# First modulation of a hybrid gMLP/HGRN2 layer: from four passes of 2 MB weight tiles to four chunks of 512 features, with the first projection interleaved

## The reference, cut to what matters

```
sh1, sc1, ... = split(silu(c) @ w_ada + b_ada, 6)       # c for latent, c_ctx for context
h_lat = rms_norm(x)   * gain * (1 + sc1)  + sh1
h_ctx = rms_norm(ctx) * gain * (1 + csc1) + csh1
U, V, Q, I, FF, FB, G = split(h @ w_in)                   # 7 x 1024 columns
mix = concat(gmlp(U, V), hgrn2(Q, I, FF, FB, G))          # context needs only I, FF, FB
x = x + g1 * (mix @ w_out)
x = x + g2 * (relu(h2 @ w_ff1)^2 @ w_ff2),  h2 = modulated rms_norm(x)
out = rms_norm(x) * final_gain
```

## Time and profile before

| | |
|---|---|
| median of 3 runs | 2718.37 us (2716.9 to 2723.17) |
| span of the profiled execution | 2717.8 us |
| TensorE busy | 2563.4 us (94%) |
| GpSimd busy | 1000.9 us (37%) |
| VectorE busy | 1246.9 us (46%) |
| ScalarE busy | 727.6 us (27%) |
| moved | 354.70 MB, mean 131 GB/s |

### The profile page before, as it was taken

One profiled execution on the slowest core, in us unless ns is written; L12 is line 12 of the kernel. 1 busy time (PEld: TensorE's weight loads), 2 busy tenths in 40 slices (PEclk: granted clock), 3 DMA queues, 4 the chain that ended last, 5 costly groups with the idle time before them and its releaser, 6 DMA issues.

```text
span 2717.8 us, 33317 instructions
## 1 busy us (share of the span) xinstructions
PE 2563.4 (94%) x12240; PEld 2111.8 (78%) x12240; DVE 1246.9 (46%) x1463; ACT 727.6 (27%) x929; POOL 1000.9 (37%) x420
## 2 busy tenths in 40 slices
PE   4789999999999999998899999999999999999997
PEld 0479787777777887787788888888888888888886
DVE  0476447788888523666423223332332333323224
ACT  1344222222222223223321322212222222231222
POOL 0330243323232343343344444444444444444442
PEclk9899999999999999999999999999999999999998
DMA  9734454333443452364133323232322322232322
GB/s 411 279 121 163 165 192 150 131 123 123 134 144 124 141 208 93 114 229 153 62 101 109 101 93 102 93 101 94 99 96 97 98 94 100 94 101 93 102 93 101
DMA packets 104769, 354.70 MB, mean 131 GB/s; under 512 B 9936, under 2 KB 10192, under 8 KB 100688
## 3 DMA queue, kind: packets, MB, share of 16 engines
q1 hardware_dynamic: 104224, 352.46, 38.1%
q10 hardware_dynamic: 432, 0.54, 0.1%
HBM read 348.77 MB, written 4.19 MB: 130 GB/s over the span
## 4 chain that ended last, share of the span: by engine, by line
PE 55%; issue 29%; POOL 10%; DMA 3%; DVE 2%; ACT 1%; POOLq 0%; SPq 0%; DVEq 0%; ACTq 0%
POOL w_lo L313 10%; PE bank L1108 9%; PE bank L1109 9%; PE bank L1110 9%; PE bank L1122 9%; PE bank L1123 9%; PE bank L1124 9%; DMA ada_w<-in_w_ada 3%; DVE prep_tmp L669 0%; DVE x_tok L659 0%; DVE x_res L1056 0%; PE bank L1068 0%; ACT junk L393 0%; DVE g_tmp L1034 0%; PE bank L1157 0%
## 5 line engine op out<-in xcount | busy, mean ns | idle before, releaser
L313 POOL TENSOR_TENSOR w_lo<-raw,w_hi 128x1024 fp32r<-128x1024 f32 x416 | 1000.7, 2406 | 1691.7 <-ACT w_hi L346 1691.7
L346 ACT ACTIVATE w_hi<-raw 128x1024 fp32r<-128x1024 f32 x448 | 475.5, 1062 | 1681.4 <-PE bank L1110 870.9
L1108 PE MATMUL bank<-h_hi,w_hi 128*128 128x512 f32 x1696 | 673.6, 397 | 3.4 <-POOL w_lo L313 2.9
L1109 PE MATMUL bank<-h_lo,w_hi 128*128 128x512 f32 x1696 | 663.7, 391 | 0.0
L1110 PE MATMUL bank<-h_hi,w_lo 128*128 128x512 f32 x1696 | 663.6, 391 | 0.0
L1122 PE MATMUL bank<-w_hi,hid_hi 128*128 128x512 f32 x1024 | 398.3, 389 | 0.0
L1123 PE MATMUL bank<-w_lo,hid_hi 128*128 128x512 f32 x1024 | 398.3, 389 | 0.0
L1124 PE MATMUL bank<-w_hi,hid_lo 128*128 128x512 f32 x1024 | 398.3, 389 | 0.0
L1108 PEld LDWEIGHTS bank<-h_hi,w_hi 128*128 128x128 f32 x1696 | 321.1, 189 | 69.8 <-POOL w_lo L313 3.4
L1110 PEld LDWEIGHTS bank<-h_hi,w_lo 128*128 128x128 f32 x1696 | 320.4, 189 | 68.0
L1109 PEld LDWEIGHTS bank<-h_lo,w_hi 128*128 128x128 f32 x1696 | 321.2, 189 | 63.6
(11 more groups left out here) (182 smaller groups left out, 2089.0 us busy)
## 6 DMA issues: line engine op xcount, KB each, us to landing
raw<-in_w_stream SPq DMA_DIRECT2D x448, 512.0 KB, 3.5
ada_w<-in_w_ada SPq DMA_DIRECT2D x128, 512.0 KB, 4.1
ada_w<-in_w_ada SPq DMA_DIRECT2D x16, 2048.0 KB, 18.0
x_tok<-in_x SPq DMA_DIRECT2D x4, 1024.0 KB, 27.1
x_res<-in_x SPq DMA_DIRECT2D x4, 1024.0 KB, 12.1
out<-x_res SPq DMA_DIRECT2D x4, 1024.0 KB, 4.0
ctx_tok<-in_ctx_x SPq DMA_DIRECT2D x2, 1024.0 KB, 16.5
fin_row<-in_final_row SPq DMA_DIRECT2D x1, 1024.0 KB, 7.0
```

The lines of the kernel that those rows point to most:

```text
L313: pool.tensor_tensor(w_lo[:, r % 2], raw[:, r], w_hi[:, r % 2].bitcast(F32), ALU.subtract).then_inc(lo_done, 1)
L346: act.activation(w_hi[:, r % 2], raw[:, r], ACT.Copy).then_inc(hi_done, 1)
L1108: pe.matmul(dst, wh, hi[:, kt], start=(kt == 0), stop=False)
L1109: pe.matmul(dst, wh, lo[:, kt], start=False, stop=False)
```

## The change

The 32 MB of w_ada are read in another order: four chunks j of 512 shift and the same 512 scale features, each chunk as 16 K tiles of 512 KB (two segments of 2 KB a row) into eight buffers. The tokens, latent and context, are loaded ahead of them, normed, and turned at once into `x_turned` and `c_turned_in`. Chunk 0 is summed by `ada1_quad` (four K tiles, eight matmuls, one bank), then `ada1_pick` and `modulation(0)` give the modulation of four K tiles of features. These four are modulated from the turned tokens (`in_act`, `in_dve`) and go at once into the projection I[:, :512] for latent and context tokens together, 18 matmuls a K tile into six open banks (`in_part`), with the quads of chunk j+1 between them. The wide units of I are thus used once for both kinds of tokens (`U_I`, 8 units), the stream is eight units (4 MB) shorter, context I[:, 512:] keeps eight wide units (`U_CTX_V`) and latent I[:, 512:] the eight tall ones (`U_V`). The low parts of units 8 to 17 are cut by VectorE. `c_turn(7)` and `c_states(7)` come after the first and the second unit of `U_V` in place of the second and the fourth, the second modulation's group 0 is added up after j = 6 of the eight units, and group 1 still after the first unit of head 0. SyncE's list issues two `load_ada2` per unit for groups 0 to 2.

```diff
+            def load_ada1(n):
+                j, k = n // KT, n % KT
+                if n >= 8:
+                    sp.wait_ge(ada1_used, (n - 8) // 4 + 1)
+                src = w_ada[k * P:(k + 1) * P, 0:4096].rearrange("p (s c) -> p s c", s=2)[:, :, 512 * j:512 * (j + 1)]
+                sp.dma_start(ada1_w[:, n % 8], src).then_inc(ada1_landed[n % 8], 16)
...
+            for j in range(CHUNKS):
+                for k in range(KT):
+                    load_ada1(KT * j + k)
+                    if j == 0 and k in (7, 9, 11, 13):
+                        load_unit(0, (k - 7) // 2, True)
+                    if j in (1, 2) and k in (7, 15):
+                        load_unit(1, 2 * (j - 1) + k // 8)
...
+            for r in range(8):
+                load_unit(U_HEADS // 4 + r // 4, r % 4)
+                for m in (6 + 2 * r, 7 + 2 * r):
+                    load_ada2(m // 8, m % 8)
...
+            for t in range(TT + CT):                       # scalar
+                act.wait_ge(token_landed[t], 16)
+                act.activation(junk_in[:], token_tile(t), ACT.Square, accum_out=stat[:, t:t + 1]).then_inc(sumsq, 1)
+                act.activation(stat[:, t:t + 1], stat[:, t:t + 1], ACT.Sqrt, bias=stat[:, 63:64], scale=1.0 / D).then_inc(root, 1)
+                if t:
+                    token_out(t - 1)
...
+            def ada1_quad(j, i):                           # tensor
+                if i == 0 and j:
+                    pe.wait_ge(ada1_rows, j)
+                for k in range(4 * i, 4 * i + 4):
+                    n = KT * j + k
+                    pe.wait_ge(ada1_landed[n % 8], 16 * (n // 8) + 16)
+                    for g in range(2):
+                        a = 2 * (k % 2) + g
+                        mm = pe.matmul(bank[6][32 * a:32 * a + 32, :], cs_wide[:, k], ada1_w[:, n % 8, g], start=(k < 2), stop=(k >= KT - 2))
+                mm.then_inc(ada1_used, 1)
...
+            for j in range(CHUNKS):
+                for g in range(8):
+                    kt = 4 * j + g // 2
+                    if j < CHUNKS - 1:
+                        if g % 2 == 0:
+                            ada1_quad(j + 1, g // 2)
+                        if g == 7:
+                            ada1_pick(j + 1)
+                    if g % 4 == 0:
+                        pe.wait_ge(lo_done, U_I + kt // 2 + 1)
+                    if g % 2 == 0:
+                        pe.wait_ge(in_lo, 2 * kt + 2)
+                    mm = in_part(kt, g % 2)
...
-            for j in range(16):
+            for j in range(8):                             # U_V
                 pe.wait_ge(lo_done, U_V + j + 1)
...
+                tall(j % 4, j % 2, bank[4 + j // 2][:], h_hi, h_lo).then_inc(unit_used, 1)
...
+                if j == 6:
                     ada2_colsum(0, 3)
```

More of the change, by code:

```diff
@@ L228, in _ @@
         def _(sp):
[L229 to L232, removed]
-            sp.dma_start(col[:], cols).then_inc(cols_landed, 16)
[L235 to L239, removed]
+            def load_ada1(n):
[4 more added lines that the diff above has]
+                sp.dma_start(ada1_w[:, n % 8], src).then_inc(ada1_landed[n % 8], 16)
+            sp.dma_start(col[:], cols).then_inc(cols_landed, 16)
+            for t in range(TT):
+                sp.dma_start(x_tok[:, t], x[t * P:(t + 1) * P, :]).then_inc(token_landed[t], 16)
+            for t in range(CT):
+                sp.dma_start(ctx_tok[:, t], ctx_x[t * P:(t + 1) * P, :]).then_inc(token_landed[TT + t], 16)
             def load_unit(q, r, first=False):
@@ L250, in load_ada2 @@
                 sp.dma_start(dst[:, m % 2], src.rearrange("(t p) c -> p t c", p=P)).then_inc(ada_landed[m % 2], 16)
[L252 to L261, removed]
+            for j in range(CHUNKS):
[5 more added lines that the diff above has]
+                        load_unit(1, 2 * (j - 1) + k // 8)
+            with sp.Fori(2, U_V // 4) as q:
                 for r in range(4):
@@ L404, in c_ktok_out @@
+            hi_unit(U_CTX_HEADS // 4, 0)
+            hi_unit(U_CTX_HEADS // 4, 1)
+            for t in range(CT):
+                act.wait_ge(unit_used, U_CTX_V + 8)
+                act.activation(v_ctx[:, t, 512:1024], bank[6 + t][:], ACT.Copy).then_inc(cv_read, 1)
             def c_ktok_out(h):
@@ L638, in _ @@
+            dve.wait_ge(turned_act, 2 * (TT + CT))
+            for j in range(CHUNKS):
+                modulation(j)
+                for m in range(8 * j, 8 * j + 8):
+                    in_dve(m)
+            dve.wait_ge(small_landed, 32)
             dve.tensor_copy(mask[:], mask_f32[:]).then_inc(mask_ready, 1)
@@ L1062, in _ @@
             pe.wait_ge(cs_ready, 2)
-            for k in range(KT):
-                pe.wait_ge(ada1_landed[k % 4], 16 * (k // 4) + 16)
-                for g in range(8):
-                    rows = slice(32 * (g % 4), 32 * (g % 4) + 32)
-                    mm = pe.matmul(bank[g // 4][rows, :], cs_wide[:, k], ada1_w[:, k % 4, g * 512:(g + 1) * 512],
-                                   start=(k == 0), stop=(k == KT - 1))
-                mm.then_inc(ada1_used if k < KT - 1 else ada1_done, 1)
@@ new lines, in ada1_pick @@
+            def ada1_pick(j):
+                if j == 0:
+                    pe.wait_ge(pick_ready, 1)
+                pe.wait_ge(ada1_rows, j + 1)
+                for i in range(4):
+                    mm = pe.matmul(bank[7][:, 16 * j + 4 * i:16 * j + 4 * i + 4], ada1_row[:, i * P:(i + 1) * P],
+                                   pick[:].rearrange("p s c -> p (s c)"), start=True, stop=True)
+                mm.then_inc(ada1_cols, 1)
+            for i in range(4):
+                ada1_quad(0, i)
```

317 lines of the change are left out of this document (167 added, 150 removed).

## The result

The changed kernel takes 2695.32 us in the median of 4 runs (2693.91 to 2698.38), the kernel before 2717.64 beside it. The ratio is 0.9912, with a 95% interval of 0.9901 to 0.9924: it is faster by 22 us. The profiled executions differ by 23.2 us (2717.8 less 2694.6), where 37.7 were forecast. The time lies in the predicted range, but 14 us above the forecast, and the size of the gain is the thing to explain.

The account below looks back on a forecast made before the run. TensorE is busy for 94% of 2717.8 us, so only its waits in the first 389 us can yield time. Step 5 brings 3.8 us, step 6 33.9, the rest nothing: 37.7, so 2681 us, range 2662 to 2704.

Parts of the forecast that it names:

- step 1: Tokens loaded first and turned: ScalarE's 3.6 us a tile is slower than landing; transposes end at about 33 us.
- step 2: Chunk 0: 512 KB transfers at 350 GB/s, 1.50 us each; landed at 53.6 us, projection begins at 61.
- step 3: Four interleaved chunks: TensorE sets the pace by a hair, 24.9 us a chunk; stage ends at 153.5 us.
- steps 4, 5: Context I's second half takes 23.5 us, to 177.0; the first context head takes 12, to 189.0.
- step 5: Context heads: first head done at 189.0 us instead of 192.8, V0 used at 286.0; brings 3.8 us.
- step 6: Latent I and second modulation: new 14 us wait at head 0, old wait goes; 33.9 us less.
- main case: The whole forecast of 2681 us, with its own range of 2668 to 2693; chance 0.54.
- Transfers that set the pace: Rival for the first stage: 2 KB segments go at 300 GB/s, stage ends 17 us later, 2698; chance 0.18.
- the slower one at 221: Rival for the first stage: transfers at 221 GB/s, 2.37 us each, stage ends 60 us later, 2741; chance 0.05.
- Hand-overs inside a chunk: Rival in the interleaved chunks: waits between engines show, 16 K tiles add 21 us, 2702; chance 0.13.
- No new wait: Rival at head 0: groups 0 and 1 run faster or TensorE arrives later, 16.6 us less, 2664; chance 0.10.

Follow-up runs that it names:

- after_late: The changed kernel with group 1's column sums of the second modulation moved from behind the first to behind the fifth unit of head 0: 2694.7 us.
- after_four: The changed kernel with four buffers instead of two for groups 0 and 1, and group 0 added up two units earlier: 2690.15 us.
- after_pad24: The changed kernel with six one-column matmuls (24 machine instructions) put at the head of TensorE's program: 2673.82 us.
- after_four_j5_pad24: The changed kernel with 24 padding instructions, four buffers, group 1's transfers issued three to a unit, group 0 added up behind j = 5: 2668.63 us.
- after_pad8: The changed kernel with two small matmuls (8 machine instructions of TensorE) added ahead of the first quads: 2708.15 us.

## Why the prediction was right, and where it was wrong

The direction and the mechanism were right. By its steps, from the rows above:

| event | forecast | measured |
|---|---|---|
| transposes end (step 1) | 33 | 31.05 |
| one 512 KB transfer (step 2) | 1.50 | 1.36 |
| first projection matmul (step 2) | 61 | 57.0 |
| length of the interleaved part (step 3) | 92.5 | 93.6 |
| from there to the first head done (steps 4, 5) | 35.5 | 34.5 |
| gain at V0 (step 5) | 3.8 | 8.6 (289.84 - 281.28) |
| wait at head 0 (step 6) | 14 | 14.0 |
| gain from V0 to head 0's second unit (step 6) | 33.9 | 34.0 |
| gain there | 37.7 | 42.6 |
| everything behind | 0 | -1.7, then -17.7 in the loop |
| sum | 37.7 | 23.2 |

**What held.** Step 6 was within 0.2 us, and the 14 us wait came at the place, for the reason and with the length forecast: two buffers, each of which costs its sum and then a transfer. The reason is shown by after_late, where asking later only moved the wait, and by the kernels with four buffers: after_four cut the wait at head 0 to 0.8 us, and all waits at the column sums together to 4 or 5. The parts that the step gives for its 33.9 (43.5 less 16.6 plus 7.8) add up to 34.7; the 33.9 itself comes from 99.0 less 65.1.

**What was a little off.** Steps 1 to 5 gained 4.8 us more than forecast, of which steps 1 and 2 together account for 4.0. Tokens were 2 us earlier: TensorE's transposes of one token tile follow those of the tile before in 3.2 us (25.96 to 29.15), and not in 3.6. And 512 KB transfers with 2 KB segments go at 385 GB/s, not at 350. The row that was taken as the nearest (346 GB/s) was a mix of segments of 2 and 4 KB. The Trainium skill, "DMA: Bandwidth & Descriptors", has the fit for a single transfer that stood against the change in its section Anatomy of one DMA. By it each would have taken an estimated 3.2 us; with eight under way the trace has 1.36.

**The step that failed** stands in the prediction's first paragraph: "Everything behind 389 us is the same code before and after, so the question is when the first unit of head 0 is used", and with it "the rest nothing" in the sum. The code is the same but lies 37 instructions further on, and the loop in it is sensitive to that. It cost 17.7 us in this kernel and 18 us in the kernel before when that was moved by 35. The right answer for the sum would have been 42.6 - 1.7 - 17.7.

**What was luck.** The measured 2695.3 us lie above the main case's own range (2668 to 2693). They lie in the stated range only because its high end, 2704, was set for slower transfers and for hand-overs that show, and neither occurred. The two errors have opposite signs (up to head 0's second unit the gain was 4.9 us larger than forecast, and 19.4 us of it were lost behind), and the first took the edge off the second.

**The rivals.** Transfers that set the pace: TensorE waited for them for 6.9 us in eight waits, seven of them before chunk 0 was complete and one of 0.3 us in the first quad behind it; at 385 GB/s that case and the slower one at 221 are out. Hand-overs inside a chunk: the wait for a low part there was 0.8 us in all. No new wait: it was 14.0. The loss in the loop was no rival of the prediction; the view that would have raised it is the count of instruction packets by window, which for the kernel before gives 55 in the last 1070 us, code that had already run once.

**What stays open.** Of the 1.7 us between head 0 and the loop 1.6 are lost at one place in head 1. TensorE's timeline there, before and then after:

```profile
459.58 1.16 PE L1230 MATMUL bank<-q_meet,k_meet 128*128 128x128 f32 x8 [2.45 <-DVE q_meet L803]
```

```profile
416.96 1.90 PE L1304 MATMUL bank<-q_meet,k_meet 128*128 128x128 f32 x8 [2.46 <-DVE q_meet L845]
```

The same wait of 2.5 us stands ahead of both, and behind it the same matmuls are slower: the granted clock of the 28 us around it is 0.94, and was 1.00. Why the clock fell in one kernel and not in the other isn't shown. Between head 0's second unit and the loop after_pad24 loses 0.8 us and after_four_j5_pad24 4.8. Nor was it observed which block of instructions makes room for which.

## What to carry to other kernels

Before a gain is forecast for a change at the front of a kernel with a hardware loop behind it, count how far the loop moves, and look at the instruction queue's packets within the loop: if there are any, the loop is fetched anew in each turn and a shift of a few instructions can cost or give some 20 us here. A wait for "issue" a few instructions behind the place that a branch returns to is the sign, and a few idle instructions ahead of the loop, where the engine waits anyway, are the remedy if their number is right: 24 of them gave as much as the change itself had left, and 8 of them cost another 13 us. The profile can also put such a wait down to another engine, as in after_pad8. And when a wait sits on a producer's own loop (VectorE's sums in two buffers), a later consumer gains nothing; more buffers do, if the queue's list lets their transfers go earlier too.

## What the runs showed of the hardware

- A loop of 768 matmuls a turn (two machine instructions each, so over 1536) runs for six turns without one instruction packet at some places of the program and with nine a turn at others, by the table above.
- The wait at the first border behind the branch costs TensorE 2.2 to 4.0 us a time; behind the one of 3.8 us the granted clock was 0.50 for about 2.5 us.
- Transfers of 512 KB in 2 KB segments, up to eight under way and a few unit loads among them, ran at 382 to 385 GB/s beside TensorE at work.
- An instruction of VectorE's sums (128x512, float32) took 0.75 us, and 2.89 us when it began together with GpSimd's cut of 2.39 us.
- The 16 recorded matmuls of one 2 MB tile took 1.92 us at a granted clock of 1.00 and 3.64 us at 0.50.
